# Dealing a sample's value products in sixths around the probability turns, in a two-layer decoder step

## The reference, cut to what matters

```python
s = jnp.einsum('btkgd,bnkd->bkgtn', qg, kc).astype(F32) * ATT_SCALE + head_bias(rel_bias, d_cmp)
p_cmp = masked_softmax(s, d_cmp >= 0)
o_cmp = jnp.einsum('bkgtn,bnkd->btkgd', p_cmp, vc.astype(F32))      # compressed blocks
...
o_sel = nsa_selected(qg, k_sel, v_sel, top_idx, top_ok, qpos, rel_bias)   # selected blocks
o_win = nsa_window(qg, kw_all, offset - win_buf.shape[1], qpos, rel_bias) # sliding window
gates = jax.nn.sigmoid(gate_logits.astype(F32)).reshape(B, T, 3, ATT_KV_HEADS, ATT_GROUP, 1)
o = gates[:, :, 0] * o_cmp + gates[:, :, 1] * o_sel + gates[:, :, 2] * o_win
```

## Time and profile before

| | |
|---|---|
| time, median of 3 runs | 2566.99 us (2560.71 to 2572.98) |
| profiled execution | 2570.45 us, its span 2568.6 us |
| PE busy | 2341.1 us, 91% of the span |
| DVE, ACT busy | 1442.5 us, 503.8 us |
| granted TensorE clock, mean | 0.948 of full speed |
| the attention stage, layer 0 | 490.1 to 646.2 us |
| the attention stage, layer 1 | 1756.2 to 1909.3 us |

### The profile page before, as it was taken

One profiled execution on the slowest core, in us unless ns is written; L12 is line 12 of the kernel. 1 busy time (PEld: TensorE's weight loads), 2 busy tenths in 40 slices (PEclk: granted clock), 3 DMA queues, 4 the chain that ended last, 5 costly groups with the idle time before them and its releaser, 6 DMA issues. The chain is left out here.

```text
span 2568.6 us, 38312 instructions
## 1 busy us (share of the span) xinstructions
PE 2341.1 (91%) x13548; PEld 1974.2 (77%) x13548; DVE 1442.5 (56%) x2715; ACT 503.8 (20%) x1206; POOL 301.9 (12%) x318
## 2 busy tenths in 40 slices
PE   8996999699799899999989959986998989999996
PEld 7874999567597688788768759985767868887885
DVE  2834665545457644567738256654545665445776
ACT  1022111223422211100110221112342212110001
POOL 0600000000231111000216000000003121110010
PEclk9996999689899899999989989988999999999998
DMA  7215998244211222322042079962440103222220
GB/s 211 69 37 173 261 267 201 72 130 124 75 27 34 64 86 83 113 82 82 17 128 66 27 192 262 274 158 82 139 134 17 44 17 99 82 66 82 82 66 35
DMA packets 303370, 273.91 MB, mean 107 GB/s; under 512 B 53825, under 2 KB 298946, under 8 KB 302970
## 3 DMA queue, kind: packets, MB, share of 16 engines
q1 hardware_dynamic: 239912, 203.30, 27.6%
q10 hardware_dynamic: 63314, 68.70, 10.1%
HBM read 262.07 MB, written 18.17 MB: 109 GB/s over the span
## 5 line engine op out<-in xcount | busy, mean ns | idle before, releaser
L449 PE MATMUL psum<-xT,ring 128*128 128x272 f32 x1408 | 325.4, 394 | 14.7 <-PEq L169 14.7
L449 PEld LDWEIGHTS psum<-xT,ring 128*128 128x128 f32 x1408 | 268.5, 191 | 70.6 <-issue 15.1
L1168 DVE STREAM_TRANSPOSE turned<-ring 128x1536 f32<-128x1536 f32 x128 | 222.7, 1765 | 112.2 <-PE psum L1047 78.7
L1047 PE MATMUL psum<-turned,W 128*128 128x128 f32 x2048 | 248.6, 281 | 0.0
L1047 PEld LDWEIGHTS psum<-turned,W 128*128 128x128 f32 x2048 | 240.6, 197 | 0.0
L2548 PE MATMUL psum<-yT,HT 128*128 128x272 f32 x896 | 215.9, 398 | 0.0
L2548 PEld LDWEIGHTS psum<-yT,HT 128*128 128x128 f32 x896 | 172.9, 193 | 36.3
L2679 PE MATMUL psum<-yT,down_sum 128*128 128x272 f32 x768 | 182.3, 393 | 6.2 <-DVE down_sum L3060 4.1
L2679 PEld LDWEIGHTS psum<-yT,down_sum 128*128 128x128 f32 x768 | 145.4, 190 | 37.8 <-DVE down_sum L3060 5.0
L1037 PE MATMUL psum<-yT,turned 128*128 (+1 forms) x1024 | 123.2, 275 | 31.5 <-DVE turned L1168 31.5
L1037 PEld LDWEIGHTS psum<-yT,turned 128*128 128x128 f32 x1024 | 122.7, 196 | 32.3 <-issue 32.3
(11 more groups left out here) (543 smaller groups left out, 3781.1 us busy)
## 6 DMA issues: line engine op xcount, KB each, us to landing
ring<-in_cache_nsa_kv SPq DMA_DIRECT2D x256, 192.0 KB, 5.4
ring<-in_cache_nsa_kv ACTq DMA_DIRECT2D x256, 192.0 KB, 5.5
ring<-in_w_up SPq DMA_DIRECT2D x32, 1024.0 KB, 5.5
HT<-in_w_down SPq DMA_DIRECT2D x32, 1024.0 KB, 5.0
ring<-in_cache_nsa_kv SPq DMA_DIRECT2D x384, 64.0 KB, 1.9
ring<-in_w_in SPq DMA_DIRECT2D x20, 1024.0 KB, 5.2
ring<-in_cache_nsa_kv ACTq DMA_DIRECT2D x128, 64.0 KB, 2.2
HT<-in_w_out SPq DMA_DIRECT2D x8, 1024.0 KB, 5.0
```

Source lines behind the costliest of these rows:

```text
L449: last = pe.matmul(psum[0:w.shape[1], 2 * (t % 3) + h, 0:HALF], w, S.xT[:, k, h * HALF:(h + 1) * HALF], start=(k == 0), stop=(k == KT - 1))
L1047: last = pe.matmul(out, S.W1[:, c, j, :], turned[:, n % 2, c, :, j % 2, j // 2, :], start=(j == 0), stop=(j == 7))
L1168: dve.transpose(dst.rearrange("p c k f x (j a) -> p (c k f) j x a", a=8), cache[:, g % slots, :, :].rearrange("p j (f d) -> p f j d", d=32 ...
```

## The change

Each third is cut into two pieces, so that a part is cut into sixths: of 16 pages the pieces hold 2, 3, 3, 2, 3, 3. An iteration issues the first piece of its third where the whole third stood, ahead of the turns, and the second piece between the turns and the values. The products with new, compressed and window keys and the wait for the pages go with the first piece. The semaphore `part` rises with the last page of the sixth piece.

```diff
-            def sample_third(n):
+            def sample_piece(n, piece):
...
-                if h == 0 and third == 0:
+                if h == 0 and third == 0 and piece == 0:
...
-                if third == 0:
+                if third == 0 and piece == 0:
                     pe.wait_ge(pages[h], 16 * by_sp * (b + 1))
                     pe.wait_ge(pages_act[h], 16 * (half - by_sp) * (b + 1))
-                for t in range(half * third // 3, half * (third + 1) // 3):
+                k = 2 * third + piece
+                for t in range(half * k // 6, half * (k + 1) // 6):
                     last = pe.matmul(o, S.st_sel[:, half * h + t, cols], vsel[:, h, t, :], start=False, stop=(h == 1 and t == half - 1))
-                if third == 2:
+                if k == 5:
                     last.then_inc(s.part, 1)
...
                     if n > lag:
-                        sample_third(n - 1 - lag)
+                        sample_piece(n - 1 - lag, 0)
                     turn(n - 1)
+                    if n > lag:
+                        sample_piece(n - 1 - lag, 1)
                 if n >= 2:
                     values(n - 2)
             for n in range(N - lag, N):
-                sample_third(n)
+                for piece in range(2):
+                    sample_piece(n, piece)
```

## The result

The changed kernel takes 2576.95 us (median of 10 runs, 2572.25 to 2582.48) against 2566.55 us before (10 runs, 2560.71 to 2573.04). The ratio is 1.004, with a 95% interval of 1.0025 to 1.0054: 10.4 us slower. The forecast was 4.4 us slower. So the way was right, and the size was less than half of what came.

A forecast was written before the change was run, and what follows sets the result against it. It took the attention stage to be bound by PE in order, and by SP's issue where pages come late. Joints of 3.4 us and later release of 0.97 made 4.4 us on the median 2566.99: 2571, range 2562 to 2582.

The forecast's parts named there:

- What bounds the stage: Attention stage: bound by PE in order, except where pages come late, then by SP issuing 24 loads in about 15.7 us.
- More joints, 0.085 us a unit: PE's groups per unit: four instead of three, joints summing to 0.27 us, which is 0.085 us more per unit.
- The upper bound of 0.21: Joints in PE's queue: if one cost the whole idle time of weight loads before a turn, 0.21 us more per unit.
- rival 2: Both new joints in all 88 units: each shape change costs its whole idle time, 0.21 us a unit, unhidden; 2586; chance 0.09.
- The Trainium skill: PE's tiling changes, two to four a unit: each drains the engine; extra cost about 0.1 us, not used in the sum.
- Which units pay, 40 of 88: Units with pages, both layers: 26 and 14 on the path, the others hidden by page waits; 40 x 0.085 = 3.4 us.
- Later release: Page buffer: a part's semaphore rises later by the turns' length, delaying SP's next 12 loads at four places; 0.97 us.
- Earlier turns worth nothing, no room lost: Turns come 0.45 to 0.66 us earlier, leaving exponentials less room; priced at zero, at most 0.5 us per layer.
- Rival 1, the clock: Granted clock in mid-stage goes another way: 2576 or 2566; chance 0.13 upward, 0.10 downward.
- Rival 3: PE's page waits, 13.9 us, shrink as SP runs ahead; if all went, 2553; chance 0.04.
- The prediction's own signs: Unit of 12 page records near 2.93 us, 3.05 for rival 2; stages changing over 10 us at equal clock refute the forecast.

The follow-up runs named there:

- one shape: The changed kernel with a stationary operand of 128 columns in place of 16 for the sample's products, so pages, turns and values are 128*128: 2570.61 us.
- 8 and 8 and one shape: The changed kernel with the 128-column stationary operand and page loads split 8 to SP, 8 to ACT: 2566.63 us, ratio to before 0.998.
- 8 and 8: Page loads split 8 to SP and 8 to ACT in place of 12 and 4: on the kernel before 2557.18 us, on the changed kernel 2579.13 us.

## Why the prediction was right in the way and off in size

- *What bounds the stage* (PE in order, SP's issue where pages come late): right. Taking a third of SP's loads away removed every page wait and 15 us, though most of these came by the clock, which fell in the middle of the stage before and didn't without page waits.
- *More joints, 0.085 us a unit*: this step failed. It measured 0.29 us in the unit at width 512, and 0.24 as a mean over 88. In the sum's own terms, turns to pages, pages to values, values to pages and pages to turns were put at 0.035, 0.10, 0.035 and 0.10; at 0.11 us a record (0.112 for values) they measure about 0.15, 0.10, 0.14 and 0.10. Pages to values and pages to turns were right; the two others were too low. I had left out that the group after a change of shape starts with an open weight load, which lengthens that group. The rows had it: in the earlier trace rows the fixed part of the turns held this for the entry from pages, while the values, following turns of the same shape, didn't. Moving pages between them gave the values that entry too (0.93 to 1.04), and the turns didn't lose theirs. The upper bound of 0.21, and rival 2 with the same price, were below the 0.29 for this reason.
- *The Trainium skill*, "TensorEngine Tiling (Array Packing)", section Key Properties: the engine drains when the tiling mode changes. The runs agree in the way: the cost of the cut is there with 128\*16 between 128\*128 and gone with one shape. By that rule the prediction named 0.1 us a unit; 0.29 came, so the size wasn't in it. The prediction also counted two changes in every unit before; a unit with scores has three.
- *Which units pay, 40 of 88*: the idea held, the count was too low. Of 21.4 us at equal clock, page waits gave back 7.3, so some 14 us stayed, the price of nearly 60 units at 0.24. The better clock of the profiled run took 7.1 more, which leaves the 7.1 that the stages show. Where no page waits are, the full 21 us appear.
- *Later release*: SP's second `vwin` load came at 511.07, 0.65 us later than in the earlier trace rows, where 0.16 and three joints of 0.085 had been foretold, 0.42; with joints of 0.29 it would be 1.0. It wasn't measured by itself.
- *Earlier turns worth nothing, no room lost*: right for this kernel (waits of 5.1 and 5.3 us, two a layer). It isn't free everywhere: with 8 and 8 and one shape, waits for exponentials grew by 3.7 us.
- *Rival 1, the clock*: it happened in the profiled runs, downward in layer 0 (0.34 x 20 us lost in the earlier trace rows, no such stretch after), and made the change look better than it is. How the clock of the other runs of before fell in this stage isn't known. Over whole executions the ten runs of the changed kernel have a mean granted clock of 0.951, and 66 runs of before, timed with the experiments, 0.949, so the other runs point the same way.
- *Rival 2* had the mechanism, with 0.09 of the chance; that page waits would swallow a part of it was also right. *Rival 3* came half true: the page waits did shrink, by 7.3 us, but PE's added work filled them, and the time rose, as the prediction argued against it.
- *The prediction's own signs*: 3.05 us or more for the unit was to speak for rival 2, and it was 3.14; more than 10 us in the two stages at an equal clock was to make the forecast wrong as a whole, and it was about 14. That 2577 lies near the forecast of 2571, well inside the range, is thus in part luck: a joint priced too low met a clock that gave 7 us back.

## What to carry to other kernels

Count the changes of stationary shape in PE's order before cutting a group: here two more per unit cost 0.29 us in the widest units (0.24 in the mean), as much as two and a half records, though no instruction was added. Price a joint on both sides, the gap ahead of the new group and the open first load within it, and ask for each existing group whether it is entered from its own shape. If idle time elsewhere hides such a cost, remove that idle time first: the kernel with its loads split evenly was 15 us faster without the cut and 22 us faster than with it.

## What the runs showed of the hardware

A weight load isn't pulled ahead over a change between 128\*16 and 128\*128, even where no semaphore wait stands between (0.21 us idle at entry to 128\*128, 0.17 to 128\*16). At over 1100 such joints, in the stages of the eight traces with both shapes, it starts at most 0.01 us ahead of the group's first matmul; where the shape stays it starts 0.11 us ahead in the median. Weight loads of 128 columns cost no more per page record than loads of 16, 0.11 us, when shapes don't change.

The 24 page loads of a sample, 64 KB each, keep SP's queue busy for 14.2 to 17.7 us before, some 0.6 us each, of which the DMA instruction itself is 0.33 (median). This, not the bandwidth, made pages late: the stages moved 122 to 125 GB/s with page waits and, with 8 and 8, 128 to 133 GB/s without any in the uncut kernels.

The granted clock is 0.50 from 5 to 15 us after the start of the stage, in both layers of all twelve traces; PE waits for its first exponentials there. In the middle of the stage it falls again, to between 0.50 and 0.86 in windows of 5 us, in 10 of the 14 stages with page waits, and in none of the 10 stages without. In the kernel before, two page waits lie in the 10 us ahead of that fall, of 2.5 and 1.8 us in layer 0 and of 2.3 and 2.2 us in layer 1.
